# Modulation sums folded to 64 partitions, split, and added by one stacked product

## The reference

```
mod = (c_act @ w_ada[l] + b_ada[l]).reshape(B, 9, 1024)
h   = rms_norm(x, gain) * (1 + mod[scale]) + mod[shift]
x   = x + mod[gate] * sublayer(h)
```

## Time and profile before

| what | us |
|---|---|
| median of 3 runs | 2667.78 |
| lowest and highest | 2667.44, 2669.97 |
| span of the profiled execution (first to last instruction) | 2663.0 |
| TensorE busy in the span | 2633.4 |
| VectorE busy | 1988.3 |
| ScalarE busy | 1302.4 |

### The profile page before, as it was taken

How to read it: one execution, slowest core, us unless ns; L and a number is a source line. 1 busy time by engine, 2 the same in 40 slices (tenths; PEclk the granted TensorE clock), 3 DMA queues, 4 the chain that set the end, 5 groups by cost and what they waited for, 6 DMA issues and landing times.

```text
span 2663.0 us, 34176 instructions
## 1 busy us (share of the span) xinstructions
PE 2633.4 (99%) x13939; PEld 2213.9 (83%) x13939; DVE 1988.3 (75%) x2258; ACT 1302.4 (49%) x1458; POOL 0.8 (0%) x6
## 2 busy tenths in 40 slices
PE   7999999999999999999999999999999999999998
PEld 5878877888888877888888899888888889997887
DVE  7767888777768888867777767777777785767744
ACT  4444566444435566544544534554454454446443
POOL 0000000000000000000000000000000000000000
PEclk9999999999999999999999999999999999999999
DMA  9886865777777874677677758548768767774752
GB/s 317 307 300 226 286 204 175 244 257 249 260 281 253 293 235 151 230 259 272 223 259 267 256 196 280 180 141 290 262 214 276 269 224 258 236 236 131 245 197 87
DMA packets 324643, 634.21 MB, mean 238 GB/s; under 512 B 12418, under 2 KB 92482, under 8 KB 324488
## 3 DMA queue, kind: packets, MB, share of 16 engines
q1 hardware_dynamic: 311952, 620.78, 67.8%
q10 hardware_dynamic: 12536, 11.25, 1.5%
HBM read 630.88 MB, written 8.97 MB: 240 GB/s over the span
## 4 chain that ended last, share of the span: by engine, by line
PE 90%; DVE 5%; DMA 3%; issue 1%; ACT 1%; SPq 0%; DVEq 0%; ACTq 0%
PE bank L1530 19%; PE bank L1532 19%; PE bank L1531 19%; PE acc L1530 8%; PE acc L1532 8%; PE acc L1531 8%; DMA raw<-in_ffn_up_all 2%; PE bank L1654 1%; DVE w_both L1009 1%; DMA raw<-in_ffn_gate_all 1%; PE bank L1591 1%; PE bank L1825 1%; DVE softmax L1232 1%; ACT w_both L581 1%; DMA x<-in_x 1%
## 5 line engine op out<-in xcount | busy, mean ns | idle before, releaser
L1009 DVE TENSOR_TENSOR w_both<-raw,w_both 128x2048 fp32r<-128x2048 f32 x412 | 942.0, 2289 | 448.2 <-ACT w_both L581 448.0
L581 ACT ACTIVATE w_both<-raw 128x2048 fp32r<-128x2048 f32 x412 | 786.5, 1912 | 535.6 <-PE bank L1532 312.3
L1530 PE MATMUL bank<-w_both,h 128*128 128x512 f32 (+1 forms) x2016 | 772.3, 383 | 5.9 <-DVE y L1153 3.8
L1532 PE MATMUL bank<-w_both,h 128*128 128x512 f32 (+1 forms) x2016 | 758.7, 376 | 0.0
L1531 PE MATMUL bank<-w_both,h 128*128 128x512 f32 (+1 forms) x2016 | 757.6, 376 | 0.0
L1530 PEld LDWEIGHTS bank<-w_both,h 128*128 128x128 f32 x2016 | 379.6, 188 | 78.0 <-DVE y L1153 4.9
L1532 PEld LDWEIGHTS bank<-w_both,h 128*128 128x128 f32 x2016 | 379.3, 188 | 70.5
L1531 PEld LDWEIGHTS bank<-w_both,h 128*128 128x128 f32 x2016 | 379.9, 188 | 66.4 <-issue 1.0
L1043 DVE SCALAR_TENSOR_TENSOR ada_sum<-raw,c_act,ada_sum 128x512 f32<-128x512 f32 x476 | 357.5, 751 | 15.4 <-DMA raw<-in_w_ada_all 1.3
L1530 PE MATMUL acc<-w_both,y 128*128 128x512 f32 x896 | 353.7, 395 | 0.0
L1532 PE MATMUL acc<-w_both,y 128*128 128x512 f32 x896 | 349.5, 390 | 0.0
(11 more groups left out here) (215 smaller groups left out, 2354.2 us busy)
## 6 DMA issues: line engine op xcount, KB each, us to landing
raw<-in_w_ada_all SPq DMA_DIRECT2D x136, 1024.0 KB, 5.2
raw<-in_w_in SPq DMA_DIRECT2D x128, 1024.0 KB, 5.4
raw<-in_ffn_gate_all SPq DMA_DIRECT2D x88, 1024.0 KB, 5.2
raw<-in_ffn_up_all SPq DMA_DIRECT2D x88, 1024.0 KB, 5.5
raw<-in_ffn_down_all SPq DMA_DIRECT2D x88, 1024.0 KB, 5.0
raw<-in_w_branch SPq DMA_DIRECT2D x12, 1024.0 KB, 7.0
first_w<-in_w_ada_all SPq DMA_DIRECT2D x8, 1024.0 KB, 14.4
raw<-in_w_out SPq DMA_DIRECT2D x8, 1024.0 KB, 5.0
```

The costliest lines, as they stand in the source:

```text
L581: activate(halves_of[n][0], src, ACT.Copy).then_inc(high_ready.sem, 1)
L1009: tensor(halves_of[n][1], raw_of("unit", s, k, 0)[0], halves_of[n][0].bitcast(F32), ALU.subtract).then_inc(low_ready.sem, 1)
L1530: mm(dst, a_h, b_h, start=start, stop=False, skip_group_check=True)
L1532: return mm(dst, a_l, b_h, start=False, stop=True, skip_group_check=True)
```

## The change

Pairs in `SPLIT` are first folded from 128 to 64 partitions: ScalarE copies the upper 64 partitions of `ada_sum` to a tile `moved` at partitions 0 to 63, and VectorE adds it to the lower 64. Then the folded sum is split: ScalarE rounds it into partitions 0 to 63 of one tile, and VectorE puts the rest into partitions 64 to 127 of the same tile. One product with ones over the 128 partitions then adds upper and lower parts together. The copy and the fold stand where round and rest stood, behind the unit after the second half; round and rest move one unit later. Pair 0 of mixer A joins `SPLIT`. `HALVES_AT` and `ADA_AT` stay.

```diff
-SPLIT = {"f": (0, 1, 2, 3, 4, 5), "a": (1, 2, 3), "b": (0, 1, 2, 3, 4, 5)}
+SPLIT = {"f": (0, 1, 2, 3, 4, 5), "a": (0, 1, 2, 3), "b": (0, 1, 2, 3, 4, 5)}
...
-        def splits_behind(s, k):
+        def splits_behind(s, k, units):
-            return [p for p in SPLIT[STAGES[s]] if p < len(ada_pairs(s)) and HALVES_AT[STAGES[s]][p][1] + 1 == k]
+            return [p for p in SPLIT[STAGES[s]] if p < len(ada_pairs(s)) and HALVES_AT[STAGES[s]][p][1] + units == k]
...
# ScalarE, in high(s, k)
-                for p in splits_behind(s, k):
+                for p in splits_behind(s, k, 1):
...
+                    if STAGES[s] == "a" and p == 0:
+                        wait_used(s, 0)
                     act.wait_ge(ada_used.sem, ada_used.at(s, p))
                     act.wait_ge(ada_part.sem, ada_part.at(s, 8 * p + 8))
-                    activate(ada_pieces(s, p)[0], ada_sum[:, :], ACT.Copy).then_inc(ada_high_ready.sem, 1)
+                    activate(ada_moved_at(s, p), ada_sum[64:P, :], ACT.Copy).then_inc(ada_moved.sem, 1)
+                for p in splits_behind(s, k, 2):
+                    act.wait_ge(ada_folded.sem, ada_folded.at(s, split_number(s, p)))
+                    activate(ada_pieces(s, p)[0], ada_sum[0:64, :], ACT.Copy).then_inc(ada_high_ready.sem, 1)
...
# VectorE, in low(s, k)
-                for p in splits_behind(s, k):
-                    high_part, low_part = ada_pieces(s, p)
+                for p in splits_behind(s, k, 1):
+                    dve.wait_ge(ada_moved.sem, ada_moved.at(s, split_number(s, p)))
+                    tensor(ada_sum[0:64, :], ada_sum[0:64, :], ada_moved_at(s, p), ALU.add).then_inc(ada_folded.sem, 1)
+                for p in splits_behind(s, k, 2):
+                    high_part, low_part, _ = ada_pieces(s, p)
                     dve.wait_ge(ada_high_ready.sem, ada_high_ready.at(s, split_number(s, p)))
-                    tensor(low_part, ada_sum[:, :], high_part.bitcast(F32), ALU.subtract).then_inc(ada_split.sem, 1)
+                    tensor(low_part, ada_sum[0:64, :], high_part.bitcast(F32), ALU.subtract).then_inc(ada_split.sem, 1)
...
# TensorE, in ada(s, k)
-                    high_part, low_part = ada_pieces(s, p)
-                    mm(ada_bank(s, p), ones_r[:, 0:1].to_broadcast([P, P]), high_part, start=True, stop=False, skip_group_check=True)
-                    last = mm(ada_bank(s, p), ones_r[:, 0:1].to_broadcast([P, P]), low_part, start=False, stop=True,
+                    both_parts = ada_pieces(s, p)[2]
+                    last = mm(ada_bank(s, p), ones_r[:, 0:1].to_broadcast([P, P]), both_parts, start=True, stop=True,
                               skip_group_check=True)
```

More of the change, by code:

```diff
@@ L167, in build @@
         bias_t = sb("bias_t", [P, 2, 768])
-        ada_in_bias = nc.alloc_sbuf_tensor_at("ada_in_bias", [P, 2, 512], F32R, offset=bias_at)
-        ada_in_y = nc.alloc_sbuf_tensor_at("ada_in_y", [P, 2, 512], F32R, offset=y_at + 4 * 2 * S * 4)
+        ada_in_bias = nc.alloc_sbuf_tensor_at("ada_in_bias", [P, 512], F32R, offset=bias_at)
+        moved_in_bias = nc.alloc_sbuf_tensor_at("moved_in_bias", [P, 512], F32, offset=bias_at + 4 * 512)
+        ada_in_y = nc.alloc_sbuf_tensor_at("ada_in_y", [P, 512], F32R, offset=y_at + 4 * 2 * S * 4)
+        moved_in_y = nc.alloc_sbuf_tensor_at("moved_in_y", [P, 512], F32, offset=y_at + 4 * 2 * S * 4 + 4 * 512)
         const = sb("const", [P, CONSTS])
@@ L262, in build, with ada_in_y_at, ada_moved_at @@
         turned = [acc[:, 1536:1920], stat[:, 0:384]]
+        def ada_in_y_at(s, p):
+            return STAGES[s] == "a" or (STAGES[s] == "b" and p >= 4)
         def ada_pieces(s, p):
-            place = ada_in_y if STAGES[s] == "a" or (STAGES[s] == "b" and p >= 4) else ada_in_bias
-            return place[:, 0, :], place[:, 1, :]
+            place = ada_in_y if ada_in_y_at(s, p) else ada_in_bias
+            return place[0:64, :], place[64:P, :], place[:, :]
+        def ada_moved_at(s, p):
+            return (moved_in_y if ada_in_y_at(s, p) else moved_in_bias)[0:64, :]
         def split_number(s, p):
             return SPLIT[STAGES[s]].index(p) + 1
-        def splits_behind(s, k):
-            return [p for p in SPLIT[STAGES[s]] if p < len(ada_pairs(s)) and HALVES_AT[STAGES[s]][p][1] + 1 == k]
+        def splits_behind(s, k, units):
+            return [p for p in SPLIT[STAGES[s]] if p < len(ada_pairs(s)) and HALVES_AT[STAGES[s]][p][1] + units == k]
         def ada_bank(s, p):
@@ L312, in build @@
         ada_used = signal("ada_used", 6, 6, 6)
-        ada_high_ready = signal("ada_high_ready", 6, 3, 6)
-        ada_split = signal("ada_split", 6, 3, 6)
+        ada_moved = signal("ada_moved", 6, 4, 6)
+        ada_folded = signal("ada_folded", 6, 4, 6)
+        ada_high_ready = signal("ada_high_ready", 6, 4, 6)
+        ada_split = signal("ada_split", 6, 4, 6)
         mod_ready = signal("mod_ready", 6, 6, 6, 2)
```

## The result

| kernel | median us | runs | profiled span us |
|---|---|---|---|
| before | 2667.78 (2667.44 to 2671.71) | 5 | 2663.0 |
| changed | 2686.59 (2680.9 to 2688.35) | 5 | 2679.1 |

The ratio is 1.0063, 95% interval 1.0052 to 1.0074: slower, as forecast, but by 18.8 us and not 8.8, and 3.6 us outside the stated range. A second measurement, beside its own runs of the kernel before (median 2668.11), gave 2683.82 us and a ratio of 1.0055 (1.0042 to 1.0067).

The account below looks back on a forecast made before the run. TensorE, busy 2633.4 of 2663.0 us, was taken as the bound. Kept savings of 14.6 us, waits of 20.0 and clock of 3.4 gave +8.8 on the 2667.8 us median: 2676.6 us, range 2668.5 to 2683.

Parts of the forecast that it names:

- What bounds it: TensorE, busy 2633.4 of 2663.0 us: nearly every matmul removed is time removed, every wait put before it time added.
- What is removed: 62 twin products of 0.23 us, plus 1.3 us at pair 0 of mixer A: 15.6 us, of which 14.6 kept.
- What is added to ScalarE and VectorE: A second instruction on each engine for 64 pairs, some 40 and 44 us, spread over idle time: costed at nothing.
- The moved step: Parts ready one unit later: TensorE waits 19.2 us in mixer A, 20.0 with slow first matmuls; none elsewhere.
- The clock: Clock falls behind both stops at pair 0 of mixer A, 3.5 us at half speed each: 3.4 us together.
- The base: Forecast counted from the 2667.8 us median, which stands 4.8 us above the profiled span of 2663.0 us.
- the clock stays up: Rival, chance 0.19: stops in mixer A occur but no clock fall follows; +5.4 us, 2673.2 us.
- head start: Rival, chance 0.10: after pair 0's stop other engines are ahead, so pairs 1 to 3 no longer wait; 2669.1 us.
- the product is passed by: Rival, chance 0.08: TensorE's queue lets unit 5's matmuls run past the waiting product in mixer A; 2653.2 us.
- VectorE gets too full: Rival, chance 0.08: later lows in feed-forwards make TensorE wait there too, 11 us more; 2687.6 us.

Follow-up runs that it names:

- Filling the stops: Changed kernel plus idle matmuls, results unused, before the products of pairs 0, 1 and 3 of mixer A: 2675.97 us; beside the changed kernel 2677.10 against 2683.82.
- the one with pair 0 back: Changed kernel with pair 0 of mixer A back on its one plain fp32 product, all else as changed: 2668.89 us, ratio to before 1.0003.
- the one with pair 0 filled: Changed kernel with 20 idle matmuls in the stop at pair 0 of mixer A alone: 2678.55 us, ratio to before 1.0032.
- half-unit-later kernel: Changed kernel with mixer A's pair 0 product behind unit 7, pairs 1, 2 and 3 in the middle of units 9, 13 and 17: 2654.81 us, ratio 0.9958.
- a whole unit: Changed kernel with mixer A's products of pairs 0 to 3 behind units 7, 9, 13, 17 instead of 4, 8, 12, 16: 2667.57 us, ratio 0.9997.

## Why the prediction was half right

- *What bounds it.* Right. TensorE paid for every stop and kept nearly every removed matmul.
- *What is removed*, 14.6 us kept: 12.5 measured (interval 8 to 15), when nothing stops. The feed-forwards with six pairs behind the first stage gave 0.9 to 1.5 each against 1.4 expected. Right within the measurement, if 2 us high.
- *What is added to ScalarE and VectorE*, nothing: right, and the guess that 64 partitions take as long as 128 came true, though the row on 8 partitions by 256 could not show it.
- *The moved step*, the main term: right in places and in size. Forecast were 7.0 and 5.3 us at pair 0, 1.1 to 1.3 at pair 1, 0.04 at pair 2 and 2.2 at pair 3; the gaps, less the regular 0.23, are 5.5, 6.0, 1.3, 0.4 and 2.4, and 19.6 in all against 19.2 (20.0 with the slow first matmuls). That the sum is closer than its parts is luck: 1.5 too much at one pair 0, 0.7 too little at the other. That feed-forwards and mixer B would not wait was right as well.
- *The clock*: this step failed. It was priced at 3.4 us, one short stretch behind each stop at pair 0. The first profile has three stretches in mixer A with 6.8 us lost, the second four with 18.7 us of busy TensorE, so 9.4 lost. Filling the stops saved 6.7 us side by side, 10.6 otherwise, and 9.1 in mixer A by the profiles. Two things were wrong in the step. The stretch length was taken from the single one in the trace, 3.5 us; of the seven behind mixer A's stops in these two profiles, five are 6.8 us long. And the stops at pair 3 were given no fall. They are the same 2.6 us from start to start in the changed kernel, in the one with pair 0 back and in the one with pair 0 filled, and in five of eight cases a fall followed.
- *The base.* "The median stands 4.8 us above that span" took one execution's luck for a constant; 1.8 of it lies outside the span, and 3.0 is how far that execution lies under the median. The second profile of the kernel before is 4.3 us longer, 3.8 of it in the first stage. As the forecast counts from the median, this moves no term of its sum, but it shows by how much a single profile can mislead. The lower end of the range does not follow from the lower ends of the terms either: 15.6 kept, 14 of waits and no fall give 2666.2 us and not 2668.5.

The sum with what was measured: -12.5 + 19.6 + 6.7 = 13.8 us, with 9.1 for the clock 16.2. The profiles give nearly the same by stages: -10.2 and -9.5 in the nine stages that are neither the first nor a mixer A, +24.4 and +27.1 in the two mixers A, so 14.2 and 17.6. The changed kernel is 15.7 and 18.8 us over the one before in its two measurements. Some 2 to 3 us stay open. The first stage swings by more than that by itself: it took 198.8 and 202.6 us in two profiles of the kernel before, and 200.5 and 198.5 in two of the changed one. So of the 10 us by which the forecast fell short of the first measurement, 3 to 6 are the clock, 2 the saving, and what is left is open.

The rivals: "the clock stays up" is refuted by its stretches; "head start" by gaps of 1.5 and 2.6 us that came back at pairs 1 and 3 behind a stop of 6; "the product is passed by" by a queue in which nothing ran ahead; "VectorE gets too full" by the half-unit-later kernel, which has every added instruction and is 12.5 us faster than before.

## What to carry to other kernels

Where one engine is busy 99% of the span, price a change by when its inputs are ready against when it wants them, product by product; a rest that was ready one unit later cost more than 62 removed matmuls gave. Then look for the place where the consumer can be moved by as much, and check what its result is waited for by: at pair 1 half a unit later was right, a whole unit made a new stop. Price a stop on TensorE with the slow matmuls behind it, by all stretches of the clock that several profiles show and not by one.

## What had not been expected of the hardware

At these lengths of idle time the length does not decide alone whether the clock falls. Equal gaps of 2.6 us at pair 3 were followed by half speed in five of eight cases, for 6.8 or 3.4 us, and not in the other three. In the first stage the thirteen profiles have ten falls, behind gaps of 3.0 to 5.9 us from start to start, and three gaps of 3.4, 3.4 and 3.8 us without one. What else decides is not shown.

The falls go with the spread of the times. In the first measurement the execution of the changed kernel with a mean granted clock of 0.994 took 2680.9 us, that with 0.993 2683.8, those with 0.992 2686.6 to 2688.4. In the second the order is looser: 0.993 went with 2682.09 and 2683.44, 0.994 with 2683.82, 0.992 with 2685.04 and 2685.2. So one profiled execution is one draw: two or three profiles of the same kernel are worth taking before a fall of the clock, or its absence, is put into a sum.
